# Paired weight loads, eight activation blocks kept in SBUF, and a new schedule for heads, gates and gathered rows in a retrieval kernel

## What is computed

```python
def block(tb):
    n = tb.shape[0]
    qv = (tb @ wq).reshape(n, PEER_HEADS, 2, PEER_HALF)
    s = jnp.einsum('thcd,hckd->thck', qv, sub_keys).astype(jnp.float32)
    s_top, i_top = lax.top_k(s, PEER_TOPK)
    ...
    best, pos = lax.top_k(cand, PEER_TOPK)
    idx = jnp.take_along_axis(cand_idx, pos, axis=-1)
    g = jax.nn.softmax(best, axis=-1).astype(tb.dtype)
    u = expert_u[idx]
    act = jax.nn.gelu(jnp.einsum('td,thkd->thk', tb, u))
    v = expert_v[idx]
    return jnp.einsum('thk,thkd->td', g * act, v)
```

## Time and profile before

| | us |
|---|---|
| median of 3 runs | 1911.04 |
| lowest, highest | 1910.48, 1920.91 |
| the profiled execution | 1913.67 |
| its span, first to last instruction | 1911.9 |

### The profile page before, as it was taken

The page is one execution under the profiler, slowest core; times in us unless marked ns, Lnnn a source line. Parts: engine busy times, 40 slices in busy tenths (PEclk is TensorE's granted clock), DMA queues, the critical chain, the costliest instruction groups (busy, mean ns, idle before and its releaser), DMA issues.

```text
span 1911.9 us, 29712 instructions
## 1 busy us (share of the span) xinstructions
PE 1802.4 (94%) x11394; PEld 1738.7 (91%) x11394; DVE 1487.0 (78%) x2660; ACT 858.2 (45%) x1272; POOL 518.3 (27%) x415
## 2 busy tenths in 40 slices
PE   5999989997999999999999999699999999999996
PEld 4999987787999999999999999699999999988995
DVE  5736597567568778999999999588888788787777
ACT  4557673223333333437777777333233233232263
POOL 2200120000000002244444444444444444434300
PEclk9999999999999999999999999899999999999998
DMA  3222333114334446789999999999999999998611
GB/s 131 78 69 78 110 99 116 68 56 165 125 125 133 154 172 213 242 282 348 365 374 364 351 359 360 387 387 376 374 365 385 382 383 382 349 342 319 209 56 47
DMA packets 163915, 462.67 MB, mean 242 GB/s; under 512 B 16640, under 2 KB 76736, under 8 KB 161216
## 3 DMA queue, kind: packets, MB, share of 16 engines
q1 hardware_dynamic: 117696, 293.00, 42.4%
q0 software_dynamic: 46080, 167.79, 23.4%
HBM read 405.46 MB, written 55.27 MB: 241 GB/s over the span
## 4 chain that ended last, share of the span: by engine, by line
PE 69%; DVE 14%; DMA 11%; ACT 3%; issue 2%; SPq 0%; DVEq 0%; ACTq 0%
PE PS L448 11%; DMA Rw<-vn 9%; PE PS L1469 8%; PE PS L1470 8%; PE PS L1471 8%; PE PS L1482 5%; PE PS L1483 5%; PE PS L1484 5%; PE PS L1458 5%; PE PS L1535 4%; PE PS L2041 2%; DVE Hl L1845 2%; ACT Rh L164 1%; DVE Rl L169 1%; DVE ug L1853 1%
## 5 line engine op out<-in xcount | busy, mean ns | idle before, releaser
L169 DVE TENSOR_TENSOR Rl<-Rw,Rh 128x1024 fp32r<-128x1024 f32 x272 | 332.3, 1222 | 180.4 <-ACT Rh L164 177.1
L164 ACT CAST Rh<-Rw 128x1024 fp32r<-128x1024 f32 x272 | 284.2, 1045 | 393.6 <-PE PS L1484 342.1
L1424 POOL DMA_INDIRECT ug<-un,idxU x160 | 240.1, 1501 | 577.3 <-DVE dots L1853 351.1
L1482 PE MATMUL PS<-Hh,Rh 128*128 128x384 f32 x1024 | 353.5, 345 | 40.0 <-DVE Hl L1845 40.0
L1469 PE MATMUL PS<-Xh,Rh 128*128 128x384 f32 x1016 | 351.2, 346 | 3.8 <-DVE Rl L169 2.8
L1483 PE MATMUL PS<-Hl,Rh 128*128 128x384 f32 x1024 | 350.6, 342 | 0.0
L1484 PE MATMUL PS<-Hh,Rl 128*128 128x384 f32 x1024 | 350.2, 342 | 0.0
L1470 PE MATMUL PS<-Xl,Rh 128*128 128x384 f32 x1016 | 342.3, 337 | 0.0
L1471 PE MATMUL PS<-Xh,Rl 128*128 128x384 f32 x1016 | 341.3, 336 | 0.0
L1424 POOL DMA_INDIRECT ug<-vn,idxU x160 | 234.4, 1465 | 287.0 <-DVE yacc L1858 222.8
L1482 PEld LDWEIGHTS PS<-Hh,Rh 128*128 128x128 f32 x1024 | 196.0, 191 | 49.5 <-issue 49.3
(11 more groups left out here) (430 smaller groups left out, 3139.6 us busy)
## 6 DMA issues: line engine op xcount, KB each, us to landing
Rw<-uw SPq DMA_DIRECT2D x144, 512.0 KB, 5.0
Rw<-vn SPq DMA_DIRECT2D x128, 512.0 KB, 7.8
Wr<-wm SPq DMA_DIRECT2D x51, 512.0 KB, 3.3
acts<-Ab SPq DMA_DIRECT2D x128, 192.0 KB, 5.4
gates<-stg SPq DMA_DIRECT2D x12, 2048.0 KB, 9.4
Gq<-gates SPq DMA_DIRECT2D x16, 1536.0 KB, 13.1
Aq<-acts SPq DMA_DIRECT2D x32, 768.0 KB, 9.2
L<-acsd SPq DMA_DIRECT2D x4, 1024.0 KB, 7.8
```

Of the source, the lines that this page charges most:

```text
L164: a.copy(self.Rh[:, q, :], self.Rw[:, q, :]).then_inc(self.S("rhi"), 1)
L169: v.tensor_tensor(self.Rl[:, q, :], self.Rw[:, q, :], self.Rh[:, q, :].bitcast(F32), ALU.subtract).then_inc(self.S("rlo"), 1)
L1424: p.indirect_dma_start(out=ug[:, r % 4, :], out_offset=None, in_=un if r < IDC else vn, in_offset=bass.IndirectOffsetOnAxis(ap=idxU[:, r % ...
L1482: pe.matmul(out, Rh[:, q, w], hh, start=(g == 0), stop=False)
```

## The change

One weight load brings two items (1 MB) from a new array `ew` that holds the weights in item order, with 8 KB in one piece for each partition. The load for items 2p and 2p+1 is issued at SP's step 2p+1 and waits for `lo(2p-3)`.

The last eight U blocks (120 to 127) write their activations straight into the first two slots of `Aq`. They are not stored or loaded. The V half takes the blocks in the order 120 to 127, 0 to 119. The array `acts` is laid out so that a load of four blocks reads 6 KB in one piece for each partition (1.5 KB before).

`load_g(0)` and one `load_a` now stand at SP's step 146; before, `load_g(0)` and three `load_a` stood at step 147.

The first four heads come every five items. Of a head's six top-k parts the fourth and fifth now share an item. The look-up groups start at items 24 and 54 (before 29 and 63), do one block in each item, and raise `sx` six items after their start. `TURN` moves from 77 to 63, the gate units from items 79 to 139 to items 65 to 134 (`GEND` 135). `ROWS` is new.

```diff
-HEAD_AT = [0, 6, 12, 18, 34, 40, 46, 52]
-LOOK = [29, 63]
+HEAD_AT = [0, 5, 10, 15, 27, 33, 39, 45]
+LOOK = [24, 54]
...
+UKEEP = PK - 8
...
-    def load(self, sp, m):
-        q = m % 4
-        if m >= 4:
-            sp.wait_ge(self.S("rhi"), m - 3)
-            sp.wait_ge(self.S("rlo"), m - 3)
-        src = self.uw[m, :, :, :].rearrange("p k j -> p (k j)") if m < NIT else self.vn[(m - NIT) * P:(m - NIT + 1) * P, :]
-        sp.dma_start(self.Rw[:, q, :], src).then_inc(self.S("rw%d" % q), 16)
+    def load(self, sp, p):
+        if p >= 2:
+            sp.wait_ge(self.S("rhi"), 2 * p - 2)
+            sp.wait_ge(self.S("rlo"), 2 * p - 2)
+        q = p % 2
+        sp.dma_start(self.Rw[:, 2 * q:2 * q + 2, :], self.ew[p, :, :, :]).then_inc(self.S("rw%d" % q), 16)
...
-    acts = nc.dram_tensor("acts", [PK, P, DT], F32, kind="Internal").ap()
+    acts = nc.dram_tensor("acts", [PK // 4, P, 4, DT], F32, kind="Internal").ap()
...
-    TURN = 77
-    G0 = 79
-    GEND = 139
+    TURN = 63
+    G0 = 65
+    GEND = 135
+
+    def v_block(g):
+
+        return (g + UKEEP) % PK
...
-    ROWS = [(46, 0), (78, 36), (VI - 1, 146), (NALL - 5, 2 * IDC)]
+    ROWS = [(32, 0), (54, 22), (64, 24), (GEND - 1, 154), (GEND + 6, 156), (NIT + 3, 164), (NALL - 5, 2 * IDC)]
...
-            if n >= 0 and u_of(n) is not None:
+            if n >= 0 and u_of(n) is not None and u_of(n) < UKEEP:
                 store_act(u_of(n))
...
-            if m < NALL:
-                ring.load(sp, m)
-            if n == GEND:
+            if m < NALL and m % 2 == 1:
+                ring.load(sp, m // 2)
+            if n == GEND + 3:
...
                 load_g(0)
-                for i in range(3):
-                    load_a(i)
+                load_a(2)
...
-            need(a, "as%d" % (g % 4), 16 * (g // 4))
-            a.activation(Ab[:, g % 4, :], PS[:, g % 2, 0:DT], ACT.Gelu_apprx_tanh).then_inc(S("glu"), 1)
+            if g == UKEEP:
+                a.wait_ge(S("gmm"), NU)
+            if g < UKEEP:
+                need(a, "as%d" % (g % 4), 16 * (g // 4))
+            out = Ab[:, g % 4, :] if g < UKEEP else Aq[:, (g - UKEEP) // 4, g % 4, :]
+            a.activation(out, PS[:, g % 2, 0:DT], ACT.Gelu_apprx_tanh).then_inc(S("glu"), 1)
...
-            v.wait_ge(S("aq%d" % (i % 3)), 16 * (i // 3 + 1))
+            if i < 2:
+                v.wait_ge(S("glu"), UKEEP + 4 * i + 4)
+            else:
+                v.wait_ge(S("aq%d" % (i % 3)), 16 * (i // 3 + (1 if i % 3 == 2 else 0)))
...
-            for part in range(6):
-                if head_at(n, 5 + part) is not None:
-                    topk(head_at(n, 5 + part), part)
+            for part, at in enumerate((5, 6, 7, 8, 8, 9)):
+                if head_at(n, at) is not None:
+                    topk(head_at(n, at), part)
...
-                if 1 <= step < 9 and step % 2 == 1:
-                    lookup(g, step // 2)
-                if step == 8:
+                if step == 1:
+                    lookup(g, 0)
+                if step == 2:
                     lookup(g, NDB)
-                if step == 9:
+                if step == 3:
                     softmax(g)
+                if 4 <= step < 7:
+                    lookup(g, step - 3)
+                if step == 6:
+                    v.wait_ge(tc, ntc[0])
+                    v.sem_inc(S("sx"), 1)
```

More of the change, by code:

```diff
@@ L143, with __init__ @@
 class Ring:
-    def __init__(self, nc, sh, uw, vn, start):
-        self.S, self.uw, self.vn = sh.sem, uw, vn
+    def __init__(self, nc, sh, ew, start):
+        self.S, self.ew = sh.sem, ew
         (self.Rw, self.Rh, self.Rl), self.end = plan(
             nc, start, ("Rw", [P, 4, D], F32), ("Rh", [P, 4, D], F32R), ("Rl", [P, 4, D], F32R))
-    def load(self, sp, m):
-        q = m % 4
-        if m >= 4:
-            sp.wait_ge(self.S("rhi"), m - 3)
-            sp.wait_ge(self.S("rlo"), m - 3)
-        src = self.uw[m, :, :, :].rearrange("p k j -> p (k j)") if m < NIT else self.vn[(m - NIT) * P:(m - NIT + 1) * P, :]
-        sp.dma_start(self.Rw[:, q, :], src).then_inc(self.S("rw%d" % q), 16)
+    def load(self, sp, p):
[4 more added lines that the diff above has]
+        sp.dma_start(self.Rw[:, 2 * q:2 * q + 2, :], self.ew[p, :, :, :]).then_inc(self.S("rw%d" % q), 16)
     def hi(self, a, m):
         q = m % 4
-        a.wait_ge(self.S("rw%d" % q), 16 * (m // 4 + 1))
+        a.wait_ge(self.S("rw%d" % (q // 2)), 16 * (m // 4 + 1))
         if m >= 4:
@@ L335, in sync @@
         sp.wait_ge(S("s0d"), 1)
-        for m in range(4):
-            ring.load(sp, m)
+        for p in range(2):
+            ring.load(sp, p)
         sp.wait_ge(S("s0d"), 1 + NB)
@@ L1365, in store_act @@
             sp.wait_ge(S("glu"), u + 1)
-            sp.dma_start(acts[u, :, :], Ab[:, u % 4, :]).then_inc(S("as%d" % (u % 4)), 16)
+            sp.dma_start(acts[u // 4, :, u % 4, :], Ab[:, u % 4, :]).then_inc(S("as%d" % (u % 4)), 16)
         def store_gates(b):
@@ L1372, in load_a @@
         def load_a(i):
+            b = v_block(4 * i) // 4
             need(sp, "hlo", i - 2)
             for s in range(4):
-                sp.wait_ge(S("as%d" % s), 16 * (i + 1))
-            sp.dma_start(Aq[:, i % 3, :, :], acts[4 * i:4 * i + 4, :, :].rearrange("i p t -> p i t")
-                         ).then_inc(S("aq%d" % (i % 3)), 16)
+                sp.wait_ge(S("as%d" % s), 16 * (b + 1))
+            sp.dma_start(Aq[:, i % 3, :, :], acts[b, :, :, :]).then_inc(S("aq%d" % (i % 3)), 16)
         def load_g(o):
             need(sp, "hfd", 2 * o - 2)
-            sp.dma_start(Gq[o % 2][:, :, :], gates[:, :, 8 * o:8 * o + 8, :].rearrange("b p i t -> p b (i t)")
+            b = v_block(8 * o)
+            sp.dma_start(Gq[o % 2][:, :, :], gates[:, :, b:b + 8, :].rearrange("b p i t -> p b (i t)")
                          ).then_inc(S("gq%d" % (o % 2)), 16)
@@ L1610, in h_hi, with sparse_act @@
             a.copy(Hh[:, i % 2, :, :], Aq[:, i % 3, :, :]).then_inc(S("hhi"), 1)
+        def sparse_act(n):
+            if rows_upto(n) >= IDC > rows_upto(n - 1):
+                a.wait_ge(S("sdt"), IDC)
+                a.activation(coef[:, :], dots[:, :], ACT.Gelu_apprx_tanh).then_inc(S("cf"), 1)
         def exps(g):
@@ L1643, in scalar @@
                 gate_out(j)
+            sparse_act(n)
             if n == NIT - 1:
@@ L1653, in scalar @@
                 h_hi(g // 4 + 1)
-            if rows_upto(n) >= IDC > rows_upto(n - 1):
-                a.wait_ge(S("sdt"), IDC)
-                a.activation(coef[:, :], dots[:, :], ACT.Gelu_apprx_tanh).then_inc(S("cf"), 1)
+            sparse_act(n)
     def vector(v):
@@ L1818, in softmax @@
             v.sem_inc(S("idx"), 1)
-            v.sem_inc(S("sx"), 1)
         def one_hot_a(j):
@@ L2242, in closing, with build @@
     return (early_sync, early_scalar, early_vector), (sync, pool, tensor, scalar, vector)
-def build(nc, x, wm, par, head, w_rg, w_ig, conv_in, s0, lru0, keys, uw, vn, un, pT, w_plg, w_plp, y, ssd_p, ssd_s, conv_o, lru_o):
+def build(nc, x, wm, par, head, w_rg, w_ig, conv_in, s0, lru0, keys, ew, vn, un, pT, w_plg, w_plp, y, ssd_p, ssd_s, conv_o, lru_o):
     with ExitStack() as ctx:
         sh = Shared(nc, ctx)
-        ring = Ring(nc, sh, uw, vn, sh.free + RING_AT)
+        ring = Ring(nc, sh, ew, sh.free + RING_AT)
         early, last = closing(nc, sh, pT, w_plg, w_plp, y)
@@ L2316, in layout @@
     u = g["peer_u"][0]
[L2317 to L2320, removed]
+    ew = np.empty((NIT + PK, P, D), np.float32)
+    ew[QITEM] = tiles(g["peer_wq"][0]).reshape(2 * PH, P, D)
+    ew[UITEM] = u.reshape(PK, PK, ND, P).transpose(0, 3, 2, 1).reshape(PK, P, D)
+    ew[NIT:] = np.roll(g["peer_v"][0].reshape(PK, PK, D), PK - UKEEP, axis=0)
+    d["ew"] = np.ascontiguousarray(ew.reshape(-1, 2, P, D).transpose(0, 2, 1, 3))
     d["un"], d["vn"] = u, g["peer_v"][0]
```

## The result

The changed kernel takes 1961.05 us (median of 4), the kernel before 1912.65 in the same comparison: a ratio of 1.0237, with a 95% interval from 1.0203 to 1.027. It is slower by 2.4%, where a small gain was forecast. The profiled execution of the changed kernel took 1949.46 us (span 1947.7), the lowest of its four. So the two traces differ by 35.8 us and the medians by 48; the last 12 us are in no trace.

What follows compares the result with a forecast made beforehand. The prediction took PE work with some 55 us of holes as the bound. Its terms, -9.6 + 6.4 + 5 - 13 = -11, with 1 for a clock dip -10, gave 1901 us from the median of 1911.04; range 1874 to 1940.

Steps and rivals of the forecast that it cites:

- Step 1: Start of the V half: PE could start at about 1226.7 instead of 1236.30, a gain of 9.6 us.
- Step 2: Heads and look-ups: PE loses 10.2 us before the turns, net loss 6.4 us; first heads at five items cost nothing.
- Step 3: Gate stretch: 1.86 rows an item and tighter DMA cost 5 us, with bounds of nothing and +27 us.
- Step 4: V half: -8 us of lateness and -5 of lowered clock, with bounds of -35 and +33.
- the term of 2.4 us: V half: gain at each gate-load group from 6 KB activation pieces beside the gathers, bounds nothing and about 2.5 us.
- The pair's 2.7 us: V half: added lateness of the pair's landing at each group with a gate load, 2.7 us at most.
- The rows' 0.6 us: V half: 0.6 us less lateness at each gate-load group, from 0.11 x 4.4 rows less.
- the pair's lead is too short: V half rival: loads come later than now if larger pieces give under 1.8 us; V +33, total +36, 1947 us; chance 0.17.
- Two rivals: Gate stretch bound by gathers or DMA rate: +27, 1923 us, chance 0.13; V half pair lead too short: 1947 us, 0.17.
- the landing of 13 to 16 us: V half sign: the first weight load behind a gate load lands 13 to 16 us after issue; 17 or more would not fit.
- the wait at the turns: Sign at `turns`: a PE wait of 5 to 10 us, released by DVE.
- The `Hl` waits below 20 us: V half sign: `Hl` waits below 20 us in total; the forecast fails if they exceed 35 us.

Runs made afterwards that it cites:

- after_single: The changed kernel with the single 512 KB weight loads of before put back, one for each item; 1909.86 us, 0.9975 to the kernel before.
- single_old_acts: after_single with the activations layout of before, loads of four blocks in 1.5 KB pieces instead of 6 KB; 1912.09 us, ratio 1.0015.
- after_one_mb_4k: The changed kernel with each pair load as one 1 MB DMA from the unpaired array, in 4 KB pieces; 1956.50 us, 1.0235 to the kernel before.

## Why the prediction was wrong, step by step

**Step 1, the start of the V half: right.** PE waits 5.88 us instead of 14.49, a gain of 8.6 us; 9.6 was forecast. The chain that remains is the one named.

**Step 2, heads and look-ups: right.** The forecast was 10.2 us lost on PE, with ACT's wait for `decode` growing to some 8. Measured: 11.4 lost, of which a part is lowered clock (0.96 in the window), and ACT's wait is 6.94:

```profile
769.23 0.43 ACT L1628 ACTIVATE tu<-tu 128x272 f32<-128x272 f32 x1 [6.94 <-DVEq L1766]
...
802.93 2.07 PE L1528 MATMUL PS<-ident,gs 128*128 128x128 f32 x9 [4.26 <-DVEq L1896]
```

PE's wait is split in two, for ACT's output and at the turns, as the sum said. The first heads at every five items can't be priced by a difference of the traces: items 2 to 49 hold other work in the two kernels (more queries and scores lie ahead of item 49 in the changed one), and no run had this edit alone. But PE has no idle time in that stretch of the changed kernel, at a granted clock of 1.00, so what was forecast to cost nothing cost PE nothing there:

```profile
488.00:735.00 247.00, 247.00 (x1633) 241.90 (x1633) 202.93 (x869) 83.36 (x127) 28.26 (x20) 1.00 0.48 164
```

**Step 3, the gate stretch: mis-sized.** Chosen were 5 us from bounds of nothing and 27; measured are 23. That this is near the upper bound is partly luck: the bound stood for a mean landing of 11.3 us, and the mean landing of the gathers in this stretch is 8.8 us, against 8.4 before and 8.5 in `after_single`. So the loss came without longer landings. The reason for staying near the low end, that POOL still waited 162 us for DVE, was no reason: in the changed kernel POOL waits 214 us for DVE, and DVE still waits 48 us for rows. The runs give the size: 11 us by the 12 rows, 13 more with the pairs. The pairs' part had stood at nothing in the sum of this stretch, without a reason. How they do it is not shown; DVE's wait for rows is 48.1 us with them and 35.3 without.

**Step 4, the V half: the wrong sign.** Forecast -13, measured +12.7 (579.5 to 592.2). The step that failed is the term of 2.4 us at each group for "the activations' share beside the gathers". The prediction itself says that no row shows it, and takes it near its upper bound; over 14 groups it is a gain of 34 us. With single loads `single_old_acts` shows 2.5 us for it in the whole V half, 0.2 at a group, and for the 8 KB pieces of the weights `after_one_mb_4k` shows no gain in the total.

The other terms came out near their size. The pair's 2.7 us at a group make 38 us, and the pairs cost 33.5 in this V half, 20 by their issue and 13 by the common landing as far as one trace of each tells. The rows' 0.6 us make 8.4, and 8.6 were measured. The sum over bytes rightly took the DMA engines for full behind a gate load (share 1.03); what it left out is that the late pair leaves them idle in front of it. With 0.2 in place of 2.4 the sum would have said 2.7 - 0.6 - 0.3 - 0.2 = 1.6 us later at each group, 22 us in all, and had the right sign. Of the 20.8 us between the V halves of the kernel before and `after_single`, rows and layout explain 11; the rest is not separated. It may lie in the kept blocks, which leave a lighter first group, and in less lowered clock. These four add up: 33.5 - 8.6 - 2.5 - 9.7 = 12.7.

The rival "the pair's lead is too short" had the sign and place, and its condition, that the larger pieces give less than 1.8 us, is what the runs show. That its +33 for the V half is close to the 33.5 that pairs cost is luck: it was set as a total against before, and that total is 12.7. Two rivals came true together: the gate stretch with 23 of its 27 us and the late loads with a V half of +12.7 where the forecast had -13. The range treated them as alternatives, and so ended at 1940. Of the signs that the prediction named, the wait at the first V item and the landing of 13 to 16 us came true; the wait at the turns was 4.3 us, with 3.7 more at ACT's output, where 5 to 10 stood. The `Hl` waits below 20 us (33.7), the DMA share near 1.0 (0.92) and the PE idle time below 10 us (15.9) did not, and with 403.6 us the gate stretch passed the 395 at which the forecast was to fail. That the Trainium skill (DMA: Bandwidth & Descriptors, Queues, rings and completion order) lets queues take turns by packets may be so; no run here shows the turns, and no clear gain of larger pieces came out of them. The Trainium skill's limit of about 358 GB/s for a core (the same page, Specifications) did not bind here: 375 GB/s were reached from 1214 to 1254 us, and 395 behind a gate load.

**The sum of the traces:** -8.6 at the V half's start, +6.9 in items 50 to 64 over the corresponding stretch before (11.4 against 94.9 - 90.4 = 4.5), +23 in the gates, +12.7 in the V half, +0.8 from the mixer, which starts the retrieval that much later. That is 34.8 of 35.8 us. The 12 us by which the median lies above the profiled execution stay open.

## What to carry to other kernels

In a ring, merging two loads halves their number, but both go out only when the second slot is free, and the first user waits for the second half's landing. Here that cost 51 us with a user close behind each load; where nobody waits close behind, it was not tried.

An average DMA share hides bursts. 0.87 over a V half is made of holes and of full stretches, and the late loads lay in the full ones. So look at the windows just before and during the wait: a sum over bytes holds where they are full, and an earlier issue helps when it fills a hole in front of them.

A term that no row shows should not decide the sign of a forecast; with its lower bound the V half's sum was a loss. And an engine with a fixed number of transfers in flight has an edge: 10% more rows an item turned no loss at all into 11 to 24 us.

## What the runs showed of the hardware that I had not expected

The size of the pieces hardly matters for the whole time between 4 KB and 8 KB for the weights (1956.5 and 1961.05 us, intervals that overlap), and between 1.5 KB and 6 KB for the activations (2.5 us in the V half). The kernel whose transfers come later ran with the lower DMA share, 0.87 and 332 GB/s in the V half against 0.94 and 352 before, at almost the same bytes, and yet at full engines (1.03 and 395 GB/s) in the bursts behind its gate loads. The mean landing of a 512 KB gather stayed between 8.3 and 8.8 us in the gate stretches of all thirteen kernels.
